# Fine score sets of the gated recurrences as four 32x32 diagonal blocks

## The reference, cut to what matters

```python
def hgrn2_scan(q, log_f, v):           # block 2; gla_mixer in block 1 has the same form
    ...
        b = jnp.cumsum(lfc, axis=1)
        diff = b[:, :, None] - b[:, None, :]
        decay = jnp.exp(jnp.where(tri[None, :, :, None, None], diff, NEG_BIG))
        attn = jnp.einsum('bhtd,btshd->bhts', qc, decay * kc[:, None])
        o_intra = jnp.einsum('bhts,bshv->bthv', attn, vc)
    ...
    return from_chunks(o)
```

## Time and profile before

| What | us |
|---|---|
| median of 3 runs | 1216.92 |
| profiled execution, its own time | 1219.77 |
| its span in the trace | 1218.0 |
| PE busy, matmuls | 1145.1 (94%) |
| DVE busy | 778.6 (64%) |
| ACT busy | 604.4 (50%) |
| DVE, splitting the weights (L280), 170 times | 388.9 |
| ACT, rounding the weights (L273), 170 times | 323.6 |

### The profile page before, as it was taken

One profiled execution on the slowest core, in us unless ns is written; L12 is line 12 of the kernel. 1 busy time (PEld: TensorE's weight loads), 2 busy tenths in 40 slices (PEclk: granted clock), 3 DMA queues, 4 the chain that ended last, 5 costly groups with the idle time before them and its releaser, 6 DMA issues. The chain is left out here.

```text
span 1218.0 us, 20514 instructions
## 1 busy us (share of the span) xinstructions
PE 1145.1 (94%) x8388; PEld 1068.7 (88%) x8388; DVE 778.6 (64%) x980; ACT 604.4 (50%) x778; POOL 0.2 (0%) x4
## 2 busy tenths in 40 slices
PE   6998999998999998989999899899998999999997
PEld 5988799987999997889898798898998798999996
DVE  6256566676555565677788544864556666777775
ACT  5454544446443435667454435545444545545553
POOL 0000000000000000000000000000000000000000
PEclk9999899999999998999999999898999999999999
DMA  8433344454555552444233133352444255555550
GB/s 303 159 105 104 138 139 156 156 184 170 181 201 172 190 189 104 146 166 139 101 127 119 70 139 138 105 173 82 162 142 168 102 181 189 195 182 175 198 178 35
DMA packets 26959, 184.69 MB, mean 152 GB/s; under 512 B 3064, under 2 KB 3592, under 8 KB 5128
## 3 DMA queue, kind: packets, MB, share of 16 engines
q1 hardware_dynamic: 26312, 181.81, 42.7%
q10 hardware_dynamic: 576, 1.85, 0.5%
HBM read 182.60 MB, written 1.05 MB: 151 GB/s over the span
## 5 line engine op out<-in xcount | busy, mean ns | idle before, releaser
L280 DVE TENSOR_TENSOR wlo<-raw,whi 128x2048 fp32r<-128x2048 f32 x170 | 388.9, 2291 | 236.1 <-ACT whi L273 232.1
L285 PE MATMUL pp<-XH,whi 128*128 128x256 f32 x1696 | 489.0, 288 | 13.2 <-DVE HF L955 8.0
L285 PE MATMUL pp<-XL,whi 128*128 128x256 f32 x1696 | 483.9, 285 | 0.0
L285 PE MATMUL pp<-XH,wlo 128*128 128x256 f32 x1696 | 483.8, 285 | 0.0
L273 ACT ACTIVATE whi<-raw 128x2048 fp32r<-128x2048 f32 x170 | 323.6, 1909 | 66.4 <-PE pp L285 48.5
L285 PEld LDWEIGHTS pp<-XH,whi 128*128 128x128 f32 x1696 | 329.9, 194 | 22.9 <-DVE HF L955 8.7
L285 PEld LDWEIGHTS pp<-XL,whi 128*128 128x128 f32 x1696 | 329.7, 194 | 0.8
L285 PEld LDWEIGHTS pp<-XH,wlo 128*128 128x128 f32 x1696 | 329.5, 194 | 0.0
L285 PE MATMUL pp<-Y,whi 128*128 128x256 f32 x480 | 87.0, 283 | 0.0
L1547 ACT ACTIVATE Y<-P 128x256 fp32r<-128x256 f32 x44 | 18.4, 418 | 132.7 <-DVE P L1580 132.7
L285 PEld LDWEIGHTS pp<-Y,whi 128*128 128x128 f32 x480 | 75.3, 192 | 0.0
(11 more groups left out here) (302 smaller groups left out, 1360.0 us busy)
## 6 DMA issues: line engine op xcount, KB each, us to landing
raw<-stream SPq DMA_DIRECT2D x170, 1024.0 KB, 4.9
P<-gains ACTq DMA_DIRECT2D x3, 512.0 KB, 3.5
X<-xt SPq DMA_DIRECT2D x2, 512.0 KB, 4.7
out<-P SPq DMA_DIRECT2D x4, 256.0 KB, 2.3
C<-consts SPq DMA_DIRECT2D x1, 761.5 KB, 12.9
P<-rows_w ACTq DMA_DIRECT2D x1, 272.0 KB, 2.8
U<-poolw SPq DMA_DIRECT2D x1, 256.0 KB, 11.8
PC<-cols SPq DMA_DIRECT2D x1, 177.0 KB, 5.6
```

Of the source, the lines that this page charges most:

```text
L280: dve.tensor_tensor(wlo[:, slot, :], raw[:, slot, :], whi[:, slot, :].bitcast(F32), ALU.subtract).then_inc(lo_ready, 1)
L285: done = pe.matmul(dst, a, b, start=first and n == 0, stop=last and n == 2, **kw)
```

## The change

Sets 0 and 4 to 8 lie within diagonal blocks of 32 tokens. PE now forms only these: each 128x128 product becomes four products of 32x32, of tokens b to b + 31 with themselves for b = 0, 32, 64, 96, written to output partitions b to b + 31 and 32 columns each. Level 3 becomes two products of 32x32 for each old one. The set of four heads and two halves is then 256 columns. DVE merges the sets in a compact tile of 128 x 256 (`diagonal`) with 32-column masks. After set 8, the compact tile is copied into the score tile, two of its row blocks by ACT and two by DVE (`spread_diagonal`), and PE waits for all four before the output products. The parts of the score tile outside the diagonal blocks are cleared beforehand by two memsets on DVE, one at the start and one early in block 2. For r = 1 and 2 the sets go round four PSUM banks, so PE waits for the set four levels back, not two. PE's wait for the norm of the recurrence before moves from level 1 to level 3. The masks shrink from 1024 to 192 columns.

```diff
-CPAST = CLEVEL + 8 * 128
+CPAST = CLEVEL + 6 * 32
...
     def level_mask(n, dt):
-        m = C[:, CLEVEL + n * 128:CLEVEL + (n + 1) * 128]
-        return (m.bitcast(dt) if dt != F32 else m).unsqueeze(1).unsqueeze(1).to_broadcast([128, 4, 2, 128])
+        at = CLEVEL + FINE.index(n) * 32
+        m = C[:, at:at + 32]
+        return (m.bitcast(dt) if dt != F32 else m).unsqueeze(1).unsqueeze(1).to_broadcast([128, 4, 2, 32])
+
+    def diagonal(r):
+        return (P[:, 40, :] if r == 0 else U[:, 14, :]).rearrange("p (h u t) -> p h u t", h=4, u=2)
+
+    def scores(r, n):
+        w = 128 if n in (1, 2) else 64
+        if r == 0:
+            at = 1024 * (n % 2)
+            return pm[:, at:at + 1024].rearrange("p (h t) -> p h t", h=4)[:, :, 0:w]
+        return bank(n % 4)[:, 0:4 * w].rearrange("p (h t) -> p h t", h=4)
+
+    def fine_scores(r, n):
+        return scores(r, n).rearrange("p h (u t) -> p h u t", u=2)
+
+    def spread_diagonal(eng, copy, r, blocks):
+        A = gated_a(gated(r)).rearrange("p (h j t) -> p h j t", h=4, j=3)
+        for j in blocks:
+            at = slice(32 * j, 32 * j + 32)
+            copy(A[at, :, 0::2, at], diagonal(r)[at, :, :, :]).then_inc(S("diagonal_spread"), 1)
...
     def gated_pe(pe, r, st):
-            if n >= 2:
-                taken_scores(pe, r, n - 2)
-            elif r:
-                taken_scores(pe, r - 1, 8)
-            if n == 1 and r:
+            ahead = 2 if r == 0 else 4
+            if n >= ahead:
+                taken_scores(pe, r, n - ahead)
+            if n == 3 and r:
                 pe.wait_ge(S("gated_y_ready"), r)
...
-                    at = slice(u * 128, u * 128 + 128)
-                    lhs, rhs = (g["k"], g["q"]) if n == 0 else (z, z)
-                    i = pe.matmul(pm[:, at_h + u * 128:at_h + u * 128 + 128], lhs[rows, tile, at],
-                                  rhs[rows, tile, at], start=True, stop=True)
+                    for b in ((0, 64) if n == 3 else (0, 32, 64, 96)):
+                        t = at + b + (32 if n == 3 else 0)
+                        i = pe.matmul(fine_scores(r, n)[b:b + 32, slot, u, :], lhs[rows, tile, at + b:at + b + 32],
+                                      rhs[rows, tile, t:t + 32], start=True, stop=True)
             i.then_inc(S("scores_ready"), 1)
-        taken_scores(pe, r, 8)
         taken_scores(pe, r, 3)
+        pe.wait_ge(S("diagonal_spread"), 4 * r + 4)
...
     def gated_act(act, r, st):
-            taken_scores(act, r, 0)
+            act.wait_ge(S("scores_cleared"), 1 if r == 0 else 2)
...
+        taken_scores(act, r, 8)
+        spread_diagonal(act, lambda out, src: act.activation(out, src, ACT.Copy), r, (2, 3))
         act.wait_ge(S("gated_o_ready"), r + 1)
...
         def take(n):
             if n == 0:
-                i = dve.tensor_tensor(A[:, :, 0::2, :], ps, level_mask(7, F32), ALU.mult)
+                if r:
+                    dve.wait_ge(S("diagonal_spread"), 4 * r)
+                i = dve.tensor_tensor(diagonal(r), fine_scores(r, n), level_mask(n, F32), ALU.mult)
             else:
-                if n == 4:
-                    taken_scores(dve, r, 3)
-                i = dve.copy_predicated(A[:, :, 0::2, :], level_mask(n - 2, I32), ps)
+                i = dve.copy_predicated(diagonal(r), level_mask(n, I32), fine_scores(r, n))
...
         take(8)
+        dve.wait_ge(S("scores_cleared"), 1 if r == 0 else 2)
+        spread_diagonal(dve, dve.tensor_copy, r, (0, 1))
...
         dve.tensor_copy(RF[:, :], zeros).then_inc(S("scalars_set"), 1)
+        dve.memset(gated_a(gated(0)), 0.0).then_inc(S("scores_cleared"), 1)
...
         rows_dve(dve, st)
+        dve.memset(gated_a(gated(1)), 0.0).then_inc(S("scores_cleared"), 1)
```

More of the change, by code:

```diff
@@ L144, in constants @@
     c[:, CIDENT:CIDENT + 128] = np.eye(128)
[L145 to L148, removed]
+    f, e = s % 32, t[:, 0:32]
+    c[:, CLEVEL:CLEVEL + 32] = f == e
+    for n, half in enumerate(LEVELS[3:]):
+        same = (f // (2 * half)) == (e // (2 * half))
+        c[:, CLEVEL + (n + 1) * 32:CLEVEL + (n + 2) * 32] = same & (f % (2 * half) < half) & (e % (2 * half) >= half)
     past = np.arange(256)[None, :]
@@ L723, in level_mask @@
     def level_mask(n, dt):
-        m = C[:, CLEVEL + n * 128:CLEVEL + (n + 1) * 128]
-        return (m.bitcast(dt) if dt != F32 else m).unsqueeze(1).unsqueeze(1).to_broadcast([128, 4, 2, 128])
+        at = CLEVEL + FINE.index(n) * 32
[16 more added lines that the diff above has]
+            copy(A[at, :, 0::2, at], diagonal(r)[at, :, :, :]).then_inc(S("diagonal_spread"), 1)
     LEVEL_SLOTS = ((1, 2, 3, 4, 5, 7), (1, 2, 3, 4, 5, 6, 7), (1, 2, 3, 4, 5, 6))
     VALUES = (W_GLA[0] - 1, BLK2 + 9, BLK2 + 13)
-    COPIED, MASKED = (1, 2, 3), (0, 4, 5, 6, 7, 8)
+    COPIED, FINE = (1, 2, 3), (0, 4, 5, 6, 7, 8)
     def taken_scores(eng, r, n):
@@ L735, in taken_scores @@
         else:
-            eng.wait_ge(S("scores_masked"), 6 * r + MASKED.index(n) + 1)
+            eng.wait_ge(S("scores_masked"), 6 * r + FINE.index(n) + 1)
     def gated_pe(pe, r, st):
@@ L751, in gated_pe @@
                 pe.wait_ge(S("gated_z_ready"), 2 * (8 * r + n))
-            if n >= 2:
-                taken_scores(pe, r, n - 2)
-            elif r:
-                taken_scores(pe, r - 1, 8)
-            if n == 1 and r:
+            ahead = 2 if r == 0 else 4
+            if n >= ahead:
+                taken_scores(pe, r, n - ahead)
+            if n == 3 and r:
                 pe.wait_ge(S("gated_y_ready"), r)
             st.go(1 if n in LEVEL_SLOTS[r] else 0)
-            b0 = 1024 * (n % 2)
-            z = g["z"][(n + 1) % 2]
+            lhs, rhs = (g["k"], g["q"]) if n == 0 else (g["z"][(n + 1) % 2],) * 2
             for h in range(4):
@@ L766, in gated_pe @@
                 rows = slice(j * g["dk"], (j + 1) * g["dk"])
-                at_h = b0 + score_slot(g, h) * 256
+                slot = score_slot(g, h)
                 if n == 1:
-                    i = pe.matmul(pm[:, at_h:at_h + 128], z[rows, tile, 0:128],
-                                  z[rows, tile, 128:256], start=True, stop=True)
+                    i = pe.matmul(scores(r, 1)[:, slot, :], lhs[rows, tile, 0:128],
+                                  rhs[rows, tile, 128:256], start=True, stop=True)
                     continue
                 for u in range(2):
+                    at = u * 128
                     if n == 2:
-                        at = u * 128
-                        i = pe.matmul(pm[0:64, at_h + at + 64:at_h + at + 128], z[rows, tile, at:at + 64],
-                                      z[rows, tile, at + 64:at + 128], start=True, stop=True)
+                        i = pe.matmul(fine_scores(r, 2)[0:64, slot, u, :], lhs[rows, tile, at:at + 64],
+                                      rhs[rows, tile, at + 64:at + 128], start=True, stop=True)
                         continue
-                    at = slice(u * 128, u * 128 + 128)
-                    lhs, rhs = (g["k"], g["q"]) if n == 0 else (z, z)
-                    i = pe.matmul(pm[:, at_h + u * 128:at_h + u * 128 + 128], lhs[rows, tile, at],
-                                  rhs[rows, tile, at], start=True, stop=True)
+                    for b in ((0, 64) if n == 3 else (0, 32, 64, 96)):
+                        t = at + b + (32 if n == 3 else 0)
+                        i = pe.matmul(fine_scores(r, n)[b:b + 32, slot, u, :], lhs[rows, tile, at + b:at + b + 32],
+                                      rhs[rows, tile, t:t + 32], start=True, stop=True)
             i.then_inc(S("scores_ready"), 1)
-        taken_scores(pe, r, 8)
         taken_scores(pe, r, 3)
+        pe.wait_ge(S("diagonal_spread"), 4 * r + 4)
         wait_evac(pe, VALUES[r])
@@ L840, in copy_scores @@
             act.wait_ge(S("scores_ready"), 9 * r + n + 1)
-            taken_scores(act, r, 0)
-            ps = pm[:, 1024 * (n % 2):1024 * (n % 2) + 1024].rearrange("p (h u t) -> p h u t", h=4, u=2)
+            act.wait_ge(S("scores_cleared"), 1 if r == 0 else 2)
             if n == 1:
-                i = act.activation(A[:, :, 1, :], ps[:, :, 0, :], ACT.Copy)
+                i = act.activation(A[:, :, 1, :], scores(r, 1), ACT.Copy)
             elif n == 2:
-                i = act.activation(A[0:64, :, 0::2, 64:128], ps[0:64, :, :, 64:128], ACT.Copy)
+                i = act.activation(A[0:64, :, 0::2, 64:128], fine_scores(r, 2)[0:64, :, :, :], ACT.Copy)
             else:
                 for at in (0, 64):
-                    i = act.activation(A[at:at + 32, :, 0::2, at + 32:at + 64], ps[at:at + 32, :, :, at + 32:at + 64], ACT.Copy)
+                    i = act.activation(A[at:at + 32, :, 0::2, at + 32:at + 64], fine_scores(r, 3)[at:at + 32, :, :, :], ACT.Copy)
             i.then_inc(S("scores_copied"), 1)
@@ L919, in gated_dve @@
         g = gated(r)
-        A = gated_a(g).rearrange("p (h j t) -> p h j t", h=4, j=3)
         def take(n):
```

(13 more changed lines are left out.)

## The result

The changed kernel took **1206.74 us** (median of 5 runs, 1205.81 to 1211.30) against 1216.94 for the kernel before in the same series: ratio 0.9915, 95% interval 0.9896 to 0.9935, or 10.2 us less.

The account below looks back on a forecast made before the run. PE's own work was taken to set the time in most steps of the three recurrences, DVE in a few. Terms +1.2, +0.9 and -0.65 summed to +1.45 us, 1218.4 in terms of the median; range 1209 to 1232.

Parts of the forecast that it names:

- the open price: PE time per record of a product with 32 columns on both sides, which no row showed; 31.6 ns taken, bounds 17 and 58.
- 31.6 ns a record: Price taken for 32-column products on PE; a fine set in the second and third recurrence goes from 1.79 to 2.02 us.
- the line: PE pitch over 128 contraction rows, from the 128x128 and 64x64 products: 4.8 ns + 0.835 ns per column.
- lower bound of 17: Lowest ns per 32-column record on PE: half of the 34 ns row with 64 contraction rows, if groups overlap.
- rival A: Four blocks run side by side on PE, 17 ns a record, fine set 1.1 us: -6.5 us, 1210.4; chance 0.33.
- upper bound of 2.02: Longest fine set forecast in the first recurrence, if heads no longer overlap; between 1.18 and 2.02 us, 1.6 taken.
- level 3 gave nothing: Second recurrence: level 3's 0.8 us is not gained, as the next pair already waits 0.17 us for DVE.
- the gaps of 0.68 and 1.30: PE idle times in the third recurrence, before the pairs after levels 5 and 4; forecast to be gone or smaller.
- rival C: PE's clock falls to half in two more places, at longer stretches without a pair: +3.3 us, 1221.5; chance 0.12.
- Idle before the output 1.5: PE's wait before the first output product of each recurrence: 1.5 us, against 1.82 in the first and 1.45 in the others.
- Two clears, constants and banks at nothing: The score tile's two clears, the shorter constants load and four PSUM banks each counted as 0 us; clears bounded by 1.6 each.
- An instruction added on PE costs its time, except in front of such a gap: Rule for the three recurrences: added PE work costs its full time unless it precedes PE idle time.

Follow-up runs that it names:

- e1_one_group: The changed kernel with all blocks of the fine sets and level 3 written to output partitions 0 to 31, one column group: 1218.46 us, ratio 1.0004.
- e8_group_runs: The changed kernel with the loop over the four 32-column blocks outermost, 16 records of one column group in a row: 1210.71 us, ratio 0.9934.
- e7_two_ahead: The changed kernel with TensorE two score sets ahead in all recurrences and the wait at level 1 again: 1208.18 us, ratio 0.9915.
- e2_blocks_only: The kernel before with only the products cut into 32x32 blocks, old places and copies of 1024 columns: 1216.79 us, ratio 0.9998.
- e5_pair_first_before: The kernel before with each level's pair of the weight stream issued ahead of the wait for that level's products: 1204.45 us, ratio 0.9887.

## Why the prediction was wrong

**The step that failed** is the open price, "Against it: no row has two column groups", and with it the choice of 31.6 ns a record laid end to end. With 128 contraction rows the line was exact (32 ns in e1_one_group, 31.6 in e8_group_runs), but it is the price within one column group. Four groups ran side by side and a record cost 9 ns, below the lower bound of 17: that bound took half of a row that already had two row groups overlapping, and did not ask for four. So a fine set was 0.76 us and not 2.02, and in the first recurrence not 1.6. The nearest rows pointed to rival A, and the argument against it was only that no row showed it.

The Trainium skill, "TensorE: Matmul & The Clock Gate", Part 3, has small-M matmuls at different output quarters run concurrently; the trace agrees, four starts in 0.03 us. The Trainium skill, "TensorEngine Tiling (Array Packing)", Instruction Overhead, has an overhead of some 60 cycles a matmul, which is 25 ns at 2.4 GHz (an estimate from that figure). Across groups the trace does not agree, with 9 ns a record; the 31.6 ns within one group lie above it and do not test it.

**Rival A by recurrence.** The second was to give 3.1 us and gave 3.0, which is partly luck: levels 5 to 8 gave 3.85, as the sets were 0.76 us and not A's 1.1, and the longer stretch at half clock took some 0.7 back. The third was to give 2.9 and gave 3.4, the first 0.5 and gave 3.4. The first was the mis-sized term: A left a set with 64 contraction rows "as long as now" (a row of 1.26 us), and the row went to 0.76, that of level 3 to 0.47. 3.4 us of PE's work came off there (46.4 to 43.0) and none of it turned into waits. There too it was the column groups: in e1_one_group, with the same order of heads, the set took 1.91 us, near the forecast's upper bound of 2.02.

**The sum by steps.** Second recurrence: level 3 gave nothing, as forecast. Its set became 1.25 us shorter and the wait before the next pair grew from 0.17 to 1.33. What was missed is that level 4's set then freed time as well, of which 0.96 us became a wait at 565.36. Third: the gaps of 0.68 and 1.30 did not go but grew, to 0.84 and 1.74, since PE came earlier by more than DVE did. There the forecast had the sign of the wait wrong, and it followed from the set's length: in e1_one_group, with sets of 2.21 us, the gap of 1.30 was 0.75, that of 0.68 was gone and that of 1.02 was 0.76. The reading left out a gap of 1.72 us in the third recurrence (before the pair of 632.95), which the change left at 1.72. Two slips in the sums are too small to matter: levels 7 and 8 of the first recurrence stand at +1.3 where twice 0.55 is 1.1, and rival C at 1221.5 where 1218.4 + 3.3 is 1221.7.

**What held.** Masked copy 0.45 forecast, 0.446 measured. Idle before the output 1.5 in all three recurrences, 1.53, 1.53 and 1.56 measured; the spread on it 0.28 twice beside 0.41 twice. Two clears, constants and banks at nothing: in e7_two_ahead no wait came back without the banks, and the runs bound them to about 1.8 us; the clears and constants were not tried apart. The rule that "An instruction added on PE costs its time, except in front of such a gap" was said of the kernel before. Between the change and e1_one_group it holds in part: 24.2 us more work in the sections, 13.3 more length, 10.8 in the ratio.

**The clock.** Rival C expected two falls more. The trace after has 14 stretches at 0.50 where 11 were, 8.2 us more in all. One of the three is at the output products of the third recurrence; the other two (at 945.0 and 1006.4) lie in a part that the change does not touch, where two stretches of before are shorter in turn. Inside the three recurrences 16.4 us ran at 0.50 where 10.2 did. So C's condition came true beside A's, though not by longer stretches without a pair: the falls stand at longer waits. It was smaller than what the overlap gave, but in e2_blocks_only the same thing took all that the blocks had gained. Which of the falls other executions have stays open, since each kernel left one profile.

## What to carry to other kernels

Products that were cut into 32 output partitions each cost 9 ns a record here when neighbours in the queue went to different column groups, and 32 ns when they did not: let the group be the innermost loop. When an engine's work is cut, look at what stands in front of its next long job: if a wait is queued there, the gain can turn into idle time, and if the long job needs nothing of that wait it should be issued first. That order was worth 14 us here, more than the change, and it costs no instruction. Judge two such cuts together as well as one by one: alone they were worth 0.2 and 3.9 us, together 10.3.

## What the hardware showed that was not expected

- With 128 contraction rows and four column groups, four records start in each 31.6 ns in the first half of a set, also where the four differ in nothing but output partitions and columns of the operands; two groups give a pitch of 16 ns.
- Within a set the second half is slower than the first. With 64 contraction rows 32 records started in 0.19 us and the last 31 between 0.24 and 0.57; with 128 rows 33 started in 0.27 us and the others again until 0.57. The second half is alike in both, about 10 ns a record, so it is hardly the array that sets it. No run isolates what does.
- With 16 records of one group in a row, the next group overlaps by some three records only. Row groups behave alike: with 64 contraction rows and long runs of one column group, a set took 0.97 us where the heads changed between the two halves every 4 records (e8_group_runs) and 1.91 where they did so every 16 (e1_one_group).
- e5_pair_first_before removed 8.9 us of waits, and two stretches at half clock, 4.1 us of busy time, went with them. That the waits brought the lower clock fits the traces and was not isolated.
